# A two-layer hybrid decoder trunk: seven block products instead of eight in the first layer's gate and up projections, with the gated activations kept in DRAM

## The chip, the cores and the metric

The kernel runs on one core of one Trainium2 chip. The core has TensorE (PE, matrix products into PSUM banks), VectorE (DVE), ScalarE (ACT), GpSimd (POOL) and SyncE (SP, which here only issues DMAs). The metric is the device time of one launch in microseconds (us).

## What is computed

The reference is one step of a two-layer decoder for a prompt of 1024 tokens and 8 single-token samples; together they are the 1032 columns (N) that every weight meets. Layer 0 mixes with a short convolution and a gated linear recurrence, layer 1 with latent attention. After each mixer stands a feed-forward stage (the FFN), and the first layer's is what the change is about:

```
def swiglu(h, w_gu, w_down):
    g, u = jnp.split(h @ w_gu, 2, axis=-1)
    return (jax.nn.silu(g) * u) @ w_down
...
hp = modulate(xp, norm_ffn[l], mp[3], mp[4])
...
xp = xp + mp[5] * swiglu(hp, w_gu[l], w_down[l])
```

Here h has 1024 features, w_gu is 1024 x 5632 (gate and up, 2816 columns each), w_down is 2816 x 1024. `modulate` is an RMS norm with a scale and a shift per feature, which come from products of a condition vector with w_ada (the "modulation" below).

## The kernel before

Everything is float32. To get float32 accuracy from TensorE's faster fp32r mode, each operand is split in a high part (a cast) and a low part (the rest), and each product is three matmuls: high by high, high by low, low by high (L2340 to L2342, function `three`). The activations lie transposed: `xT` is 128 partitions x 8 feature tiles (KT) x 1032 columns, `hh` and `hl` are high and low part of the normed input.

**How the first FFN is tiled.** The 1032 columns are three column groups (c = 0, 1, 2) of 344, one PSUM bank each (bank 0, 1, 2). The 5632 gate and up columns are 22 pairs of 128-wide tiles. A *slot* is one weight tile (128 output features) against all columns: 3 groups x 8 feature tiles x 3 matmuls = 72 matmuls of 344 columns. A pair (gate slot, up slot) is 144 matmuls; the text calls it a *tile* of the gate and up product. The stage (`ffn`, called with l = 0) goes through chunks of 6, 6, 5 and 5 tiles (FFN_CHUNKS). After the gate and up slots of a chunk come 8 *down* slots, each with n x 3 x 3 matmuls of 344 columns for the n tiles of the chunk; their result is added to `xT` by DVE (`add_to_x`, L1541 to L1547).

**Who does what in a tile.** SP loads the weights (L515). POOL splits them: cast to `whi` (L746), rest to `wlo` (L748). PE multiplies. ACT takes the gate banks with Silu (L1211), DVE multiplies by the up banks (L1915, `atmp`), ACT casts to `ahi` (L916), POOL makes `alo` (L825). All stay in SBUF. Every engine works through its own list in the order of the program and waits on semaphores; nothing is reordered at run time.

**The modulation of layer 1 rides along.** In the first 12 tiles PE also computes 24 *units* of the second layer's modulation, two in a tile: 16 small matmuls (`ada`, L2459) into bank 4 or 5, ACT copies the result to `adar` (`ada_rows`, L1041), and PE turns it with 2 matmuls each of two passes (`ada_turned`, L2468). In this kernel PE does the `ada` of a slot after column group 0 and the turning after column group 2, so ACT has two column groups of time for the copy.

**The start of the stage.** The output projection of the mixer ends in two slots whose column groups alternate (LAST_PAIR). The squares of `xT` are summed by PE against ones (L2430, L2434), ACT takes the root (L1000), DVE the reciprocal (L1507). Then DVE scales (`htmp`, L1523), ACT adds the shift and casts to `hh` (L1009, L1010), and POOL makes `hl` (L777), feature tile by feature tile; PE starts with the first.

The lines that set the turn-taking on PE are these:

```
def with_ada(i, b, c):
    if c == 0:
        ada(2 * i + 2 * f0 + b, i + f0, b, 1)
    if c == 2:
        ...
        ada_turned(2 * i + 2 * f0 + b, i + f0, b, 1)
```

## Time and profile before

| | us |
|---|---|
| median of three runs | 2955.21 |
| lowest, highest | 2953.56, 2957.14 |
| span of the profiled execution | 2954.8 |

| engine | busy, us | share of the span |
|---|---|---|
| PE, matmuls | 2868.8 | 97% |
| PE, weight loads (PEld) | 2666.3 | 90% |
| DVE | 1087.5 | 37% |
| ACT | 640.8 | 22% |
| POOL | 1037.1 | 35% |

The first FFN begins when the output projection's last product is through (652.47 us from the span's start) and ends at 1459.25 us, where the next stage's first product starts. A matmul's printed duration contains its latency and overlaps the next; how fast matmuls follow each other is read from their starts, or from a stretch's length over their count.

### The profile page before, as it was taken

How to read it: one execution, taken by the hardware profiler on the slowest of the kernel's cores; microseconds unless marked ns; L12 is line 12 of the kernel's file. 1: busy time of each engine (PE TensorE's matmuls, PEld its weight loads, DVE VectorE, ACT ScalarE, POOL GpSimd, SP SyncE). 2: the span in 40 equal slices, each digit the busy share in tenths (PEclk: the TensorE clock that was granted, in tenths of full speed). 3: DMA queues.
4: the chain of work that ended last, by engine and by line, in shares of the span. 5: the costliest groups of instructions: out<-in, count | busy, mean ns of one | idle time of the engine just before them, and what ended most of it. 6: DMA issues, size and time to landing. Idle time of an engine off the chain costs nothing.

```text
span 2954.8 us, 56225 instructions
## 1 busy us (share of the span) xinstructions
PE 2868.8 (97%) x21017; PEld 2666.3 (90%) x21017; DVE 1087.5 (37%) x2298; ACT 640.8 (22%) x1441; POOL 1037.1 (35%) x1060
## 2 busy tenths in 40 slices
PE   6999999999999999999998999999999999999999
PEld 5898998888999999999887787878789999999999
DVE  4767777321020011111436666666650110101103
ACT  5121221223101101001444333332351001000014
POOL 4000000444333334334754333333274334334344
PEclk8999999999999999999999999999999999999999
DMA  7311111453324311111232434343431111111112
GB/s 266 94 44 42 40 45 36 157 165 121 96 75 128 96 47 50 38 54 38 62 105 88 148 97 143 104 136 107 128 113 50 38 49 47 45 50 41 52 42 80
DMA packets 314743, 247.99 MB, mean 84 GB/s; under 512 B 19651, under 2 KB 299062, under 8 KB 313158
## 3 DMA queue, kind: packets, MB, share of 16 engines
q1 hardware_dynamic: 296578, 219.45, 23.9%
q10 hardware_dynamic: 9796, 17.81, 1.7%
q0 software_dynamic: 8192, 8.40, 1.0%
q8 instruction: 107, 1.75, 0.2%
q14 instruction: 70, 0.57, 0.1%
HBM read 222.87 MB, written 22.74 MB: 83 GB/s over the span
## 4 chain that ended last, share of the span: by engine, by line
PE 91%; ACT 2%; DVE 2%; POOL 1%; SPq 1%; issue 1%; DMA 1%; POOLq 0%; DVEq 0%; ACTq 0%
PE bank L2340 24%; PE bank L2342 23%; PE bank L2341 23%; PE bank L2826 2%; PE bank L2945 2%; PE bank L2847 2%; PE bank L2459 1%; POOL hl L777 1%; PE bank L2868 1%; PE bank L2608 1%; PE bank L2580 1%; PE bank L2933 1%; PE bank L2625 1%; SPq L529 1%; PE bank L2815 1%
## 5 line engine op out<-in xcount | busy, mean ns | idle before, releaser
L2340 PE MATMUL bank<-hh,whi 128*128 128x344 f32 (+1 forms) x3468 | 1141.7, 329 | 41.6 <-POOL hl L777 15.0
L2341 PE MATMUL bank<-hl,whi 128*128 128x344 f32 (+1 forms) x3468 | 1115.5, 322 | 0.0
L2342 PE MATMUL bank<-hh,wlo 128*128 128x344 f32 (+1 forms) x3468 | 1115.0, 322 | 0.0
L2340 PEld LDWEIGHTS bank<-hh,whi 128*128 128x128 f32 x3468 | 657.4, 190 | 84.0 <-issue 33.7
L2341 PEld LDWEIGHTS bank<-hl,whi 128*128 128x128 f32 x3468 | 657.3, 190 | 2.5 <-issue 1.1
L2342 PEld LDWEIGHTS bank<-hh,wlo 128*128 128x128 f32 x3468 | 657.2, 190 | 0.6
L746 POOL CAST whi<-wst 128x1024 fp32r<-128x1024 f32 (+4 forms) x222 | 180.6, 813 | 1004.0 <-PE bank L2342 721.8
L1915 DVE TENSOR_TENSOR atmp<-sil,bank 128x344 f32<-128x344 f32 x132 | 67.7, 513 | 938.5 <-PE bank L2342 924.4
L748 POOL TENSOR_TENSOR wlo<-wst,whi 128x1024 fp32r<-128x1024 f32 (+4 forms) x222 | 400.9, 1806 | 17.8
L2340 PE MATMUL bank<-ahi,whi 128*128 128x344 f32 x1056 | 338.7, 321 | 0.0
L2341 PE MATMUL bank<-alo,whi 128*128 128x344 f32 x1056 | 337.4, 319 | 0.0
L2342 PE MATMUL bank<-ahi,wlo 128*128 128x344 f32 x1056 | 337.1, 319 | 0.0
L1211 ACT ACTIVATE sil<-bank 128x344 f32<-128x344 f32 x132 | 60.4, 458 | 963.4 <-PE bank L2342 963.3
L877 POOL DMA_DIRECT2D pr<-in_cache_krope x256 | 139.2, 544 | 219.9 <-issue 215.8
L1543 DVE SCALAR_TENSOR_TENSOR xT<-bank,mod,xT 128x344 f32 (+2 forms) x216 | 123.7, 573 | 220.5 <-PE bank L2342 202.3
L2340 PEld LDWEIGHTS bank<-ahi,whi 128*128 128x128 f32 x1056 | 198.4, 188 | 0.9 <-issue 0.6
L2341 PEld LDWEIGHTS bank<-alo,whi 128*128 128x128 f32 x1056 | 198.4, 188 | 0.1
L2342 PEld LDWEIGHTS bank<-ahi,wlo 128*128 128x128 f32 x1056 | 198.2, 188 | 0.0
L758 POOL TENSOR_TENSOR hl<-xT,hh 128x344 fp32r<-128x344 f32 x24 | 22.3, 963 | 453.7 <-ACT hh L916 453.7
L825 POOL TENSOR_TENSOR alo<-atmp,ahi 128x344 f32 (+1 forms) x132 | 122.5, 929 | 158.3 <-ACT ahi L916 158.3
L916 ACT CAST ahi<-atmp 128x344 f32 (+1 forms) x132 | 63.1, 479 | 299.1 <-DVE atmp L1915 299.1
L1541 DVE TENSOR_TENSOR gtmp<-bank,mod 128x8 f32<-128x8 f32 x72 | 12.0, 167 | 236.2 <-PE bank L2342 236.1
(360 smaller groups left out, 3143.9 us busy)
## 6 DMA issues: line engine op xcount, KB each, us to landing
wst<-in_w_gu SPq DMA_DIRECT2D x88, 512.0 KB
adaw<-in_w_ada SPq DMA_DIRECT2D x40, 1024.0 KB, 5.4
pk<-in_cache_ckv SPq DMA_DIRECT2D x256, 128.0 KB, 2.4
wst<-in_w_in_even SPq DMA_DIRECT2D x28, 512.0 KB
wst<-in_w_down SPq DMA_DIRECT2D x32, 384.0 KB
wst<-in_w_down SPq DMA_DIRECT2D x32, 320.0 KB
adae<-in_w_ada SPq DMA_DIRECT2D x4, 2048.0 KB, 16.2
pr<-in_cache_krope POOLq DMA_DIRECT2D x256, 32.0 KB, 2.3
```

The source lines that it names most:

```text
L746: nc.gpsimd.tensor_copy(whi[b][:, 0:nk, :], wst[b][:, 0:nk, :]).then_inc(w_hi, 1)
L748: nc.gpsimd.tensor_tensor(wlo[b][:, 0:nk, :], wst[b][:, 0:nk, :], whi[b][:, 0:nk, :].bitcast(F), ALU.subtract).then_inc(w_split, 1)
L825: nc.gpsimd.tensor_tensor(d, atmp[c][:], one(ahi[:, bass.ds(i, 1), cols(c)]).bitcast(F), ALU.subtract).then_inc(alo_ready, 1)
L877: pool.dma_start(pr[q][:, j % CG, :], cache_krope[0, bass.ds(page, 1)].rearrange("o p c -> p (o c)")).then_inc(rope_in[q], 16)
L916: nc.scalar.copy(dst, src).then_inc(ready, 1)
L1211: nc.scalar.activation(sil[c][:], bank[c][:, 0:CW], ACT.Silu).then_inc(bank_free[c], 1)
L1543: ins = v.scalar_tensor_tensor(xc, src[:, 0:w], one(gate[:, bass.ds(m, 1), 0:1]), xc, ALU.mult, ALU.add)
L1915: v.tensor_tensor(atmp[c][:], sil[c][:], bank[c][:, 0:CW], ALU.mult).then_inc(act_ready, 1)
L2340: mm(out, wh_, xh_, start=start, stop=False)
L2341: mm(out, wh_, xl_, start=False, stop=False)
L2342: return mm(out, wl_, xh_, start=False, stop=stop)
L2826: ins = nc.tensor.transpose(bank[5][:, (2 * e + ct) * P:(2 * e + ct + 1) * P], page[:, ct * P:(ct + 1) * P], ident[:])
```

## The change

The gate and up product of the first FFN becomes a 2 x 2 x 2 block product by a scheme of Strassen's kind. The blocks of the weights are gate and up (two) by the lower and upper half of the features (two, 4 feature tiles each: KH = 4). The blocks of the activations are the two halves of the features by column *quarters* of 258 (QW = 258): for q = 0 the quarters 0 and 1, for q = 1 the quarters 2 and 3. Seven products P1, P2, P5, P6, P7, P4, P3 (in this order, each for q = 0 and q = 1) take the place of eight; each is 4 feature tiles x 3 matmuls of 258 columns. So a tile is 7 x 2 x 12 = 168 matmuls of 258 columns, where it was 144 of 344.

For that, operands are made that are sums and differences of blocks. On the activations' side this is done once, at the start of the stage, in place in `xT` (`operands` on DVE, `operand_highs` on ACT, `operand_lows` on POOL); the old `xT` is saved to DRAM before and loaded back later. On the weights' side it is done for each tile: DVE makes four sums (`weight_sum`), ACT casts seven 128x512 blocks (`op_high`), POOL makes seven low parts (`op_low`). Behind the products ACT and DVE combine the results (`p1_copy`, `u2_copy`, `u3_copy`, `g1`, `c22`, `g2`), take Silu and multiply, ACT and POOL split the result, and SP stores high and low part to DRAM (`act_high`, `act_low`). All 22 tiles are done before the down product starts; its chunks are now 2, 4, 6, 6 and 4 tiles (DOWN_CHUNKS), loaded back from DRAM (`tile_in`).

Three products share the accumulator `acc_a` (banks 0 and 1), so P7 waits until ACT has copied P6 away, and P4 until ACT has copied P7. The diff, cut to what the following sections speak of:

```
+DOWN_CHUNKS = [(0, 2), (2, 4), (6, 6), (12, 6), (18, 4)]
+QW = N // 4
+KH = KT // 2
+P1, P2, P5, P6, P7, P4, P3 = range(7)
...
+        acc_a, acc_d, acc_b = ([bank[b][:, 0:QW] for b in pair] for pair in ((0, 1), (2, 5), (4, 3)))
+        acc_q = [acc_a, acc_d, acc_b, acc_a, acc_a, acc_a, acc_b]
...
@@ SP @@
+                def cycle(t, ada=False, more=True):
+                    if more:
+                        sp.wait_ge(*op_lo(t.count(7, 7)))
+                        raw_load(l, t.next(2))
+                    for q in range(2):
+                        store(t.next(-1), q)
+                    if ada:
+                        for b in range(2):
+                            load_ada(1, t.at(2, b - 2), b)
...
@@ ACT, in out_proj and behind it @@
+                act.wait_ge(bank_ready[NC - 1], G_OUT + KT + 2)
+                for p in (P7, P4, P3):
+                    op_high(p, first)
...
+            def op_high(p, t):
+
+                if p == P1:
+                    act.wait_ge(*raw_in[t.b](t.loads()))
+                if p in MADE:
+                    act.wait_ge(*s_made(t.count(4, MADE.index(p) + 1)))
+                if not t.first:
+                    act.wait_ge(*block_done[p](t.count(2, 0)))
+                nc.scalar.copy(op_h[p][:], op_source(p, t)).then_inc(op_hi.sem, 1)
...
+                def cycle(t, ada=False, more=True):
+                    gate2(1, t.next(-1))
+                    p1_copy(0, t)
+                    act_high_half(1, 0, t.next(-1))
+                    p1_copy(1, t)
+                    act_high_half(1, 1, t.next(-1))
+                    if more:
+                        op_high(P1, t.next(1))
+                    gate1(0, t)
+                    gate1(1, t)
+                    if more:
+                        op_high(P2, t.next(1))
+                        op_high(P5, t.next(1))
+                    if ada:
+                        ada_rows(t.at(2, ADA_LAYER - 4), 0, 1)
+                    u2_copy(0, t)
+                    u2_copy(1, t)
+                    if more:
+                        op_high(P6, t.next(1))
+                    if ada:
+                        ada_rows(t.at(2, ADA_LAYER - 3), 1, 1)
+                    u3_copy(0, t)
+                    u3_copy(1, t)
+                    if more:
+                        op_high(P7, t.next(1))
+                    act_high_half(0, 0, t)
+                    if more:
+                        op_high(P4, t.next(1))
+                    act_high_half(0, 1, t)
+                    gate2(0, t)
+                    if more:
+                        op_high(P3, t.next(1))
...
+                act.dma_start(xT[:, 5:KT, 0:T], x_rest[:, 5:KT, 0:T]).then_inc(x_in[1].sem, 16)
...
@@ DVE, end of operands (q = 1), and gated @@
+                t1(*quarters[1])
+                t2(*quarters[1])
+                third_out()
+                t3(*quarters[1])
+                t4(*quarters[1])
+                lows(*quarters[1])
...
+                g1(1, t)
+                dve.wait_ge(*t_lo(2 * LOWS))
+                weight_sum(P5, t.next(1))
+                weight_sum(P7, t.next(1))
+                weight_sum(P6, t.next(1))
+                c22(1, t)
...
@@ PE @@
+                else:
+                    pe.wait_ge(*{P6: p1_out, P7: u2_out, P4: u3_out, P3: c22_sum}[p](t.count(2, q + 1)))
+                for j in range(KH):
...
+                    ins = three(acc_q[p][q], op_h[p][:, j, :], op_l[p][:, j, :], t_high[p][:, q, j, :], t_low[p][:, q, j, :],
+                                j == 0 and p in (P1, P2, P5), j == KH - 1, p in (P6, P7, P4, P3))
...
+                def cycle(t, ada_at=None):
+                    for p in range(7):
+                        for q in range(2):
+                            product(p, q, t)
+                        if ada_at is not None:
+                            a, n = t.at(2, -4), t.at(1, -2)
+                            if p == P2:
+                                ada(a, n, 0, 1)
+                            elif p == P5:
...
+                                ada_turned(a, n, 0, 1)
+                                ada(t.at(2, -3), n, 1, 1)
+                            elif p == P6:
+                                ada_turned(t.at(2, -3), n, 1, 1)
```

**How it moves instructions on PE, around a unit of the modulation.** Before, in a tile of the loop, a unit's `ada` is followed by a whole column group of products (24 matmuls) and more before `adar` is turned:

```order
L2342 MATMUL bank<-hh,wlo 128x344
L2456 REGISTER_ALU
L2459 MATMUL bank<-adaw_93,siluc 9x256 x8
L2340 MATMUL bank<-hh,whi 128x344
L2341 MATMUL bank<-hl,whi 128x344
L2342 MATMUL bank<-hh,wlo 128x344
```

Now, in a tile that carries two units (op_h_218 is the high part of P5's weights, op_h_219 of P6's, ada_x the weights of the modulation):

```order
L3038 MATMUL bank<-t_high_203,op_h_218 128x258
L3039 MATMUL bank<-t_low_210,op_h_218 128x258
L3040 MATMUL bank<-t_high_203,op_l_225 128x258
L3162 REGISTER_ALU
L3165 ISA
L3165 MATMUL bank<-sel,adar 128x9
L3165 ISA
L3165 MATMUL bank<-sel,adar 128x9
L3156 MATMUL bank<-ada_x_247,siluc 9x256 x8
L3417 REGISTER_ALU
L3422 REGISTER_ALU
L3038 MATMUL bank<-t_high_204,op_h_219 128x258
```

The first unit's turning now stands directly behind P5's last matmul, and the second unit's `ada` directly behind that.

**And on ACT, in the same place.** Before, in the loop, `adar` is copied right behind the Silu of column group 0:

```order
L1210 ISA
L1211 ACTIVATE sil_79<-bank 128x344
L1039 ISA
L1040 REGISTER_ALU
L1041 COPY adar<-bank 128x256
L1210 REGISTER_ALU
L1211 ACTIVATE sil_80<-bank 128x344
```

Now (L1558 casts the next tile's weights, L1584 copies P6's result, L1357 copies `adar`):

```order
L1558 CAST op_h_217<-raw_230 128x512
L1558 CAST op_h_218<-s_raw 128x512
L1354 ISA
L1355 REGISTER_ALU
L1357 COPY adar<-bank 128x256
L1581 REGISTER_ALU
L1583 REGISTER_ALU
L1584 COPY tq_1_237<-bank 128x258
L1581 REGISTER_ALU
L1583 REGISTER_ALU
L1584 COPY tq_1_239<-bank 128x258
L1558 CAST op_h_219<-raw_230 128x512
```

Each copy of `adar` now stands behind a cast that overwrites the weights of the product that PE has just finished (op_h_218, then op_h_219).

**And on POOL, at the start of the stage.** Before, one weight tile's split stands ahead of the first low part of the input:

```order
L746 CAST whi<-wst 128x1024
L748 TENSOR_TENSOR wlo<-wst,whi 128x1024
L777 TENSOR_TENSOR hl<-htmp_82,hh 128x344
L777 TENSOR_TENSOR hl<-htmp_83,hh 128x344
L777 TENSOR_TENSOR hl<-htmp_84,hh 128x344
```

Now (op_l_227 to op_l_229 are the low weights of P7, P4 and P3, t_low the low parts of the activations' operands):

```order
L1036 TENSOR_TENSOR op_l_227<-raw_first_233,op_h_220 128x512
L1036 TENSOR_TENSOR op_l_228<-raw_first_233,op_h_221 128x512
L1036 TENSOR_TENSOR op_l_229<-raw_first_232,op_h_222 128x512
L1049 TENSOR_TENSOR t_low_208<-xT,t_high_201 128x258 x4
L1053 TENSOR_TENSOR t_low_209<-xT,t_high_202 128x258 x4
L1059 TENSOR_TENSOR t_low_210<-xT,t_high_203 128x1032
L1061 TENSOR_TENSOR t_low_211<-t_raw,t_high_204 128x1032
L1066 TENSOR_TENSOR t_low_214<-xT,t_high_207 128x1032
```

The first low part that PE needs stands behind three low parts of weights, and three of 1032 columns stand behind the eight of 258, once for each q.

## Rows read from the trace of the kernel before

**Rows 1.** The page: the chain that ended last, share of the span by engine.

```profile
PE 91%; ACT 2%; DVE 2%; POOL 1%; SPq 1%; issue 1%; DMA 1%; POOLq 0%; DVEq 0%; ACTq 0%
```

**Rows 2.** Windows (stretch, length, then as headed) of the first FFN's gate and up.

```profile
core 0: us, PE busy (x) PEld busy (x) DVE busy (x) ACT busy (x) POOL busy (x), PEclk, DMA share, GB/s
652.47:821.57 169.10, 161.68 (x1111) 146.96 (x1109) 28.28 (x51) 44.76 (x100) 76.82 (x65) 0.99 0.32 97
889.69:1045.05 155.36, 155.36 (x1106) 145.16 (x1105) 9.72 (x21) 19.60 (x47) 55.64 (x41) 1.00 0.36 109
1113.18:1226.47 113.29, 113.29 (x722) 113.29 (x721) 8.11 (x17) 13.02 (x29) 45.75 (x34) 1.00 0.15 45
```

**Rows 3.** Timeline (start and duration in us) of PE, 256 columns, second layer.

```profile
1737.79 0.28 PE L2340 MATMUL bank<-whi,hh 128*128 128x256 f32 x1
...
1740.29 0.28 PE L2340 MATMUL bank<-whi,hh 128*128 128x256 f32 x1
```

**Rows 4.** Timeline of PE and ACT around a copy of `adar`.

```profile
709.42 0.32 PE L2342 MATMUL bank<-hh,wlo 128*128 128x344 f32 x1
...
709.86 0.46 ACT L1211 ACTIVATE sil<-bank 128x344 f32<-128x344 f32 x1 [8.29 <-PE bank L2342]
710.21 0.37 ACT L1041 COPY adar<-bank 128x256 f32<-128x256 f32 x1
```

**Rows 5.** Timeline of ACT and PE where PE waited for `adar`.

```profile
82.79 0.37 ACT L1041 COPY adar<-bank 128x256 f32<-128x256 f32 x1
...
83.31 0.36 PE L2468 MATMUL bank<-sel,adar 128*128 128x9 f32 x2 [0.86 <-ACT adar L1041]
```

**Rows 6.** Groups by line and shape: count, busy us, mean ns, idle before.

```profile
L916 ACT CAST ahi<-atmp 128x344 f32 x126 | 60.4, 479 | 291.3 <-DVE atmp L1915 291.3
L1102 ACT CAST whi<-wst 128x1024 fp32r<-128x1024 f32 x28 | 29.3, 1046 | 90.2 <-PE bank L2342 90.2
L1258 ACT COPY craw<-bank 128x344 f32<-128x344 f32 x15 | 6.6, 440 | 23.8 <-PE bank L2342 23.8
...
L1686 DVE TENSOR_TENSOR qb<-qb,hq 128x1024 f32<-128x1024 f32 x4 | 4.9, 1226 | 0.1
...
L825 POOL TENSOR_TENSOR alo<-atmp,ahi 128x344 f32 x108 | 100.1, 928 | 123.1 <-ACT ahi L916 123.1
L748 POOL TENSOR_TENSOR wlo<-wst,whi 128x512 fp32r<-128x512 f32 x4 | 5.2, 1288 | 0.3
L748 POOL TENSOR_TENSOR wlo<-wst,whi 128x1024 fp32r<-128x1024 f32 x102 | 244.1, 2393 | 8.2
```

**Rows 7.** Timeline of DVE and PE at the start of the stage.

```profile
652.40 0.42 DVE L1547 TENSOR_TENSOR xT<-xT,gtmp 128x8 f32<-128x8 f32 x1
...
653.25 3.47 DVE L1523 SCALAR_TENSOR_TENSOR htmp<-xT,amp,bank 128x344 f32<-128x344 f32 x7 [0.16 <-DVE mod L1556]
...
657.51 2.30 DVE L1507 RECIPROCAL bank<-rt 128x344 f32<-128x344 f32 x1
...
656.26 0.50 PE L2340 MATMUL bank<-hh,whi 128*128 128x344 f32 x1 [3.50 <-POOL hl L777]
656.55 0.49 PE L2341 MATMUL bank<-hl,whi 128*128 128x344 f32 x1
```

**Rows 8.** Windows, as in rows 2, of the stage's first 19 us.

```profile
656.00:660.00 4.00, 3.74 (x13) 3.22 (x14) 3.66 (x5) 4.00 (x9) 3.94 (x6) 0.57 0.00 0
660.00:675.00 15.00, 11.27 (x60) 6.81 (x59) 10.44 (x18) 11.98 (x26) 9.93 (x11) 1.00 0.37 107
```

**Rows 9.** The page's DMA issues: count, KB each, us to landing.

```profile
x_rest<-xT ACTq DMA_DIRECT2D x15, 516.0 KB, 3.0
xT<-x_rest SPq DMA_DIRECT2D x4, 1548.0 KB, 10.0
xT<-x_rest SPq DMA_DIRECT2D x5, 1032.0 KB, 5.2
```

**Rows 10.** Groups by shape: DVE's add to `xT` behind a down product.

```profile
L1543 DVE SCALAR_TENSOR_TENSOR xT<-bank,mod,xT 128x344 f32 x128 | 73.7, 576 | 175.0 <-PE bank L2342 166.3 <-DVE xT L1547 8.1 <-DVE amp L1559 0.6
```

731 lines of the change are left out of this document (652 added, 79 removed).

## The prediction, made before the changed kernel had run

> **What bounds the kernel now.** The chain that ended last is PE for 91% of the span [rows 1], so PE's time in the changed stretches decides. I read the windows of the first FFN next [rows 2]. Five tiles without modulation units take 113.29 us for 720 matmuls with PE and its weight loads busy throughout: 0.1573 us from matmul to matmul, 22.66 us a tile. Six tiles with units take 155.36 us, or 25.89 a tile, so two units cost 3.23 us of PE. The first six tiles take 169.10 us: the start of the stage costs 13.7 us over that rate. ACT, DVE and POOL are busy for an eighth to two fifths of a steady stretch. The timelines then tell how long a hand from PE to ACT and back takes, which this change puts on the path.
>
> **The products.** The trace has a run of the same fp32r triples at 256 columns: 21 matmuls in 2.50 us, 0.1190 each [rows 3]. From 256 to 344 columns that is 0.00044 us a column, so 258 columns take 0.1199. A tile is 168 x 0.1199 = 20.14 us, 2.52 less than 22.66; over 22 tiles **-55.4 us**. The bounds are close: pure proportion to the columns (0.1180) gives -62, and 0.122 gives -48. The scheme has 168 matmuls where 144 were, so it gains only while a matmul of 258 columns takes under 144/168 of one of 344, or 0.1348 us. At 256 columns the trace is well below that.
> A rule speaks against it: the Trainium skill, page "TensorE: Matmul & The Clock Gate", section "Back-to-back issue gap", gives a sustained stream of weight load and matmul as about 81 ns at 128 columns and 131 ns at 512. As an estimate from that page, 344 columns would take 109 ns and 258 columns 98 ns, a tile would go from 15.7 to 16.5 us, and the products would cost 16 us more in all. This trace disagrees at both widths (157 and 119 ns), so I go by the trace.
>
> **The steady tile, other engines.** A product of one q is 12 x 0.12 = 1.44 us. P7 of a q waits for ACT's copy of P6 of that q, and one product of the other q lies between. The hand over is: ACT starts 0.44 us after the start of PE's last matmul, 0.28 after PE would go on [rows 4]; the copy of 258 columns takes 0.37 (440 ns at 344 [rows 6], 0.37 at 256 [rows 4]); PE starts 0.15 after ACT's end [rows 5]. That is 0.80 of the 1.44 there are, so it is hidden if ACT's list is not late. Seven casts of 512 (0.62, between 479 ns at 344 and 1046 at 1024), and fourteen operations of 258 at some 0.4, are 10 us of 20; POOL's seven low parts at 1.29 and four at 0.75 are 12 us; DVE's are 7. I walked the three lists once round the tile and found no PE wait. The four DVE sums and the low parts have most of a tile of time. Cost **0**, and 0.5 to 1 us a tile if the cover of 0.64 us is gone (below). The stores and reloads of the activations (1 MB a tile each way) use a DMA that is busy for 0.36 of the time with units running [rows 2]: 0.
>
> **The units of the modulation.** This is what eats the gain. PE turns the first unit directly behind P5, and the copy that it waits for stands in ACT's list behind the cast of the next tile's P5 weights, which itself may not start before P5 of this tile is done. So PE waits: 0.28 to ACT, 0.51 from the start of the cast to that of the copy (0.62 less the 0.11 by which operations overlap: 0.46 long, 0.35 apart [rows 4]), 0.37 the copy, 0.15 back: 1.31 us. The second unit's copy stands behind the copy of P6 for q = 1 (0.26) and the cast of P6: 1.57 us. Before, a column group of 3.8 us covered this copy. In the 12 tiles with units that is 12 x 2.88 = **+34.6 us**. Bounds: 12 x 2.4 if the turning's own start is absorbed in the wait, 12 x 3.4 if ACT's register instructions add to each step: +29 to +41. A tile with units then takes 20.14 + 3.23 + 2.88 = 26.2 us, no better than the 25.9 before.
>
> **The start of the stage.** Now P1 needs only one quarter, but everything behind it is a chain over three engines. On ACT, casts for P7, P4 and P3 stand behind the last square; on POOL their low parts (3 x 1.29) push the first low part of the input to 659.1, against 656.26 [rows 7]. Then POOL sets the pace: 8 x 0.75 until P2 ends at 664.8. For P5, ACT has to finish 16 casts and shifts (0.40 each), 4 shifts and a copy before the 1032-column cast (1.05), POOL takes 2.41 for its low part: 668.9. P6 needs another 2.41. Then P7 and P4 each wait 0.8 for a copy; q = 0 ends at about 678.6. For q = 1 DVE has a reciprocal (2.30 [rows 7]) and eight scalings (0.49 apart) left, ACT follows at 0.80 a feature tile until 685.5, P2 ends at 686.7. Then POOL has two low parts of the next tile's weights ahead of the 1032-column one: P5 starts at 693.2, P6 ends at 697.0. The copy that P7 waits for stands behind ACT's cast of the next P5 weights, this behind DVE's `weight_sum`, this behind `dve.wait_ge(*t_lo(2 * LOWS))`, that is behind POOL's last 1032 columns at 697.9: P7 starts at 700.2. The tile ends at 705.4, and I add 0.6 for matmuls at half the clock behind the idle gaps: after the 3.5 us gap the clock stood at 0.57 [rows 8] and matmuls came 0.29 apart [rows 7]. Cost over a plain tile: 706.0 - 652.47 - 20.14 = 33.4, against 13.7 before: **+19.7 us**. Bounds: +8 (each link 15% shorter, the last one hidden) to +32.
>
> **The down product.** The same matmuls, so 0 in itself. With chunks of 2 a slot is 18 x 0.157 = 2.83 us, and DVE needs three adds of 0.58 [rows 10] and some 0.5 for the samples: hidden. At its start DVE is late by the last sums, the modulation's 1.2 us and so on, about 3.2 us: PE waits some 1.1 us at the second slot. Rows 5 to 7 of `xT` come back only after the last store has landed (about 3 us [rows 9]); they are 1.5 MB, and such loads took 5.2 to 10.0 us [rows 9], so they land 13 to 18 us into the down product, and slot 4 needs them at 13.4, slot 5's banks at 15.3. Together **+2 us** (1 to 5).
>
> **The sum.** -55.4 + 34.6 + 19.7 + 2 = +0.9 us on the profiled span of 2954.8, which is 0.4 below the median of the runs. So 2955.7 + 0.4 = **2956 us**. The seven-product scheme saves 55 us of matmuls and gives them back at the start of the stage and in the waits for `adar`.
>
> **Rivals.**
> 1. *The start is cheap.* If the engines' lists overlap better than in my walk, because q = 0's products already run while operands are made, the start costs +8 and the units +30: -55.4 + 30 + 8 + 2 = -15, **2940 us**. For it: ACT, DVE and POOL were busy 60 to 80% of the first 15 us [rows 8], not all of it. Against: each link that I counted is an instruction with a row. Chance 0.28.
> 2. *ACT's list is late in the steady tile* (the slower side). ACT takes casts, Silus and copies in a fixed order, and a copy of P6 or P7 that ends over 1.44 us after its product stops PE. It decides as soon as something ahead of `u2_copy` or `u3_copy` holds ACT for over 0.64 us, one cast's length. At 1 us a tile for 22 tiles this is +22: **2978 us**. For it: six hands from PE to ACT and back in 20 us where there were three in 26. Against: by my walk ACT is free before each of them. Chance 0.30, with a start of the stage at its upper bound counted here.
> 3. *The clock falls in the stage again and again.* The matmuls after the 3.5 us gap ran at 1.2 instead of 2.4 GHz; but with PE waiting half a microsecond at each feature tile afterwards the clock stood at 1.00 [rows 8]. Waits of 1.3 and 1.6 us are between. If they halve the clock for some 3 us each, it is 24 x 1.5 = +36: **2992 us**, chance 0.05.
> 4. *Matmuls of 258 columns are not cheaper* than 0.1348, from a fixed cost that 256 columns don't show: products +0, total +56: **3011 us**, chance 0.02. By the Trainium skill's figures above, the same sum would end at some 3027.
>
> **How the numbers follow.** The forecast, the parts cancelling, has 0.35. About 0.2% (5.9 us) is what a measurement of this kernel can tell from no change. Of the forecast's chance some falls on each side of that bound; with the rivals I get faster 0.31, same 0.33, slower 0.36. For the range, the bounds of the four terms (-62 to -48, 29 to 41, 8 to 32, 1 to 5) taken together give 2934 to 2983; with rival 2 inside it and rivals 3 and 4 outside, about 0.2 is left out.
>
> **What would show it.** In the profile after: (1) matmuls of 258 columns 0.119 to 0.121 us apart, and tiles without units 20.1 us each; (2) in each tile with units two PE waits for ACT `adar`, 1.3 and 1.6 us, before L3165; (3) the first tile ends about 53 us after the output projection, with PE waits of 4 us before P5 of q = 0 and 6.5 us before P5 of q = 1; (4) PE waits of 1 to 4 us in the first down chunk. A steady tile clearly over 20.2 us, waits for `tq` or `u3` in the loop, or no wait before L3165 would make it wrong.

## The result, and the profile after

| | runs | median us | range | profiled execution | its span | granted clock |
|---|---|---|---|---|---|---|
| before | 4 | 2956.18 | 2953.56 to 2957.77 | 2955.2 | 2954.8 | 0.988 |
| changed | 4 | 2998.28 | 2993.12 to 3006.16 | 3006.16 | 3004.1 | 0.975 |

The changed kernel is slower: its time is 1.0148 of before, 95% interval 1.013 to 1.0165, some 42 us where 0 were forecast, and outside the range of 2934 to 2983. The two profiled spans lie 49.3 us apart, since the profiled execution of the changed kernel is its slowest. This is how the difference spreads over the stretches of the two traces (after minus before, in us):

| stretch | forecast | traces | |
|---|---|---|---|
| output projection, before the stage | 0 | +4.8 | ends at 657.3, was 652.5 |
| products of 22 tiles | -55.4 | -53.9 | 20.21 us a plain tile, was 22.66 |
| units of the modulation, 12 tiles | +34.6 | +46.2 | 85.0 us over plain tiles, were 38.8 |
| start of the stage | +19.7 | +33.4 | 67.35 us to tile 1, less a plain tile 47.1, were 13.7 |
| down product | +2 | +16.3 | 271.98 us, was 255.72 |
| behind it | 0 | +2.4 | |
| sum | +0.9 | +49.2 | |

PE still holds most of the chain that ended last, but DVE and "issue" have doubled against [rows 1], and ACT went from 2% to 3%:

```profile
PE 87%; DVE 4%; ACT 3%; issue 2%; SPq 1%; DMA 1%; POOL 1%; DVEq 0%; ACTq 0%; POOLq 0%
```

The windows of the changed kernel, in the order first tile, twelve tiles with units, eight plain tiles, down product (compare [rows 2]):

```profile
core 0: us, PE busy (x) PEld busy (x) DVE busy (x) ACT busy (x) POOL busy (x), PEclk, DMA share, GB/s
657.30:724.65 67.35, 37.54 (x174) 34.13 (x173) 56.43 (x77) 37.03 (x74) 39.72 (x33) 0.67 0.11 36
744.96:1072.46 327.50, 293.87 (x2499) 271.77 (x2497) 97.35 (x168) 116.91 (x276) 147.89 (x132) 0.97 0.49 156
1072.46:1234.16 161.70, 161.70 (x1346) 161.70 (x1345) 61.79 (x108) 70.15 (x162) 93.02 (x86) 1.00 0.40 130
1234.16:1506.14 271.98, 258.51 (x1598) 252.79 (x1597) 104.10 (x215) 17.43 (x36) 104.86 (x103) 0.99 0.37 126
```

The third row is the part that came as forecast: PE busy throughout at clock 1.00, 161.70 us for 8 x 168 matmuls, 0.1203 each. In the first row DVE is busy for 56 of 67 us and PE for little over half, at a granted clock of 0.67: a mix of its two levels, 2.4 and 1.2 GHz. A matmul of 258 columns comes 0.12 us after the one before at the higher level and 0.215 at the lower.

Next comes the timeline of ACT and PE in a tile with units, around the second unit. ACT goes from the cast of the next tile's weights straight to the copy of `adar`, and PE, which waits for that copy, stands idle for 1.42 us. That figure starts at the printed end of PE's last matmul. The next one could have started 0.16 us earlier, so the wait costs 1.58 us; the waits of the units are counted this way below. All twelve tiles have two such waits, 37.5 us in all:

```profile
760.77 0.38 ACT L1584 COPY tq<-bank 128x258 f32<-128x258 f32 x1 [1.06 <-PE bank L3040]
761.04 0.62 ACT L1558 CAST op_h<-raw 128x512 fp32r<-128x512 f32 x1
761.56 0.38 ACT L1357 COPY adar<-bank 128x256 f32<-128x256 f32 x1
762.08 0.58 PE L3165 MATMUL bank<-sel,adar 128*128 128x9 f32 x4 [1.42 <-ACT adar L1357]
```

Now the timeline of DVE and POOL in the first tile. DVE's `t3` (L2453, four operations of 258 columns with two inputs in SBUF) takes 7.51 us beside three subtractions of POOL. By the single operations: 2.24, 2.60 and 2.42 us while POOL works, and 0.47 for the last, with POOL idle.

```profile
672.39 7.51 DVE L2453 SCALAR_TENSOR_TENSOR xT<-xT,mod 128x258 f32<-128x258 f32 x4
672.16 2.19 POOL L1059 TENSOR_TENSOR t_low<-xT,t_high 128x1032 fp32r<-128x1032 f32 x1 [3.62 <-ACT t_high L1622]
674.40 2.46 POOL L1061 TENSOR_TENSOR t_low<-t_raw,t_high 128x1032 fp32r<-128x1032 f32 x1
676.83 2.38 POOL L1066 TENSOR_TENSOR t_low<-xT,t_high 128x1032 fp32r<-128x1032 f32 x1
```

The same happens in the down product and at its end. The add of the samples' 8 columns (L2041, also two inputs in SBUF) starts after POOL's subtraction has started and ends 0.02 to 0.03 us after it, and PE waits for the add, directly or through ACT's `atmp`. With no POOL operation beside it the add takes 0.16.

```profile
1265.40 1.26 POOL L960 TENSOR_TENSOR wlo<-wst,whi 128x512 fp32r<-128x512 f32 x1
1265.48 1.20 DVE L2041 TENSOR_TENSOR xT<-xT,gtmp 128x8 f32 x1
1266.73 0.42 PE L3038 MATMUL bank<-down_high,whi 128*128 128x344 f32 x1 [1.25 <-DVE xT L2041]
...
1500.88 2.34 POOL L960 TENSOR_TENSOR wlo<-wst,whi 128x1024 fp32r<-128x1024 f32 x1
1501.28 1.97 DVE L2041 TENSOR_TENSOR xT<-xT,gtmp 128x8 f32<-128x8 f32 x1
...
1503.83 0.84 PE L3130 MATMUL bank<-atmp,ones 128*128 128x344 f32 x2 [2.49 <-ACT atmp L1245]
```

Last, the output projection, which the forecast had not looked at. SyncE's queue issues the loads of `raw_first` ahead of a load of output weights. POOL waits 12.17 us for these weights, ACT's square waits for POOL, and PE waits for the copy behind the square.

```profile
602.66 1.93 SPq L681 DMA_DIRECT2D raw_first<-in_w_gu  x2
604.71 2.71 SPq L620 DMA_DIRECT2D wst<-in_w_out_even  x1
612.91 1.04 POOL L958 CAST whi<-wst 128x1024 fp32r<-128x1024 f32 x1 [12.17 <-DMA wst<-in_w_out_even]
617.35 0.49 ACT L1245 ACTIVATE sq<-xT 128x344 f32<-128x344 f32 x1 [14.28 <-POOL acce L981]
618.46 0.61 PE L3165 MATMUL bank<-sel,adar 128*128 128x9 f32 x4 [3.52 <-ACT adar L1357]
```

### The profile page after: what moved, and what is told of

Its sections match the earlier page's. It is cut to its first block, busy times and chain, and to the rows that moved or that the text cites. A ratio compares the mean times of both kernels' runs of the same rounds, so it can differ in the third digit from the quotient of the medians.

```text
span 3004.1 us, 58789 instructions
## 1 busy us (share of the span) xinstructions
PE 2847.3 (95%) x21545; PEld 2640.4 (88%) x21545; DVE 1293.6 (43%) x2615; ACT 785.1 (26%) x1772; POOL 1105.8 (37%) x1162
## 4 chain that ended last, share of the span: by engine, by line
PE 87%; DVE 4%; ACT 3%; issue 2%; SPq 1%; DMA 1%; POOL 1%; DVEq 0%; ACTq 0%; POOLq 0%
PE bank L3038 23%; PE bank L3039 22%; PE bank L3040 22%; PE bank L3594 2%; PE bank L3713 2%; PE bank L3615 2%; PE bank L3156 1%; PE bank L3636 1%; PE bank L3305 1%; PE bank L3277 1%; PE bank L3701 1%; PE bank L3322 1%; PE bank L3165 1%; SPq L634 1%; POOL hl L989 1%
## 5 line engine op out<-in xcount | busy, mean ns | idle before, releaser
L3038 PE MATMUL bank<-hh,whi 128*128 128x344 f32 (+2 forms) x2412 | 799.7, 332 | 33.9 <-POOL wlo L960 7.7
L3039 PE MATMUL bank<-hl,whi 128*128 128x344 f32 (+2 forms) x2412 | 780.1, 323 | 0.0
L3040 PE MATMUL bank<-hh,wlo 128*128 128x344 f32 (+2 forms) x2412 | 779.9, 323 | 0.0
L3038 PEld LDWEIGHTS bank<-hh,whi 128*128 128x128 f32 (+1 forms) x2412 | 459.9, 191 | 61.3 <-issue 23.8
L3039 PEld LDWEIGHTS bank<-hl,whi 128*128 128x128 f32 (+1 forms) x2412 | 460.2, 191 | 2.4 <-issue 1.0
L3040 PEld LDWEIGHTS bank<-hh,wlo 128*128 128x128 f32 (+1 forms) x2412 | 460.4, 191 | 0.6
L3038 PE MATMUL bank<-t_high,op_h 128*128 128x258 f32 x1232 | 363.8, 295 | 29.8 <-POOL t_low L1059 11.0
L3039 PE MATMUL bank<-t_low,op_h 128*128 128x258 f32 x1232 | 357.8, 290 | 0.0
L3040 PE MATMUL bank<-t_high,op_l 128*128 128x258 f32 x1232 | 356.5, 289 | 0.0
L960 POOL TENSOR_TENSOR wlo<-wst,whi 128x1024 fp32r<-128x1024 f32 (+5 forms) x186 | 297.5, 1599 | 14.9
```

What stands on the lines that cost most here:

```text
L960: nc.gpsimd.tensor_tensor(wlo[b][:, 0:nk, :], wst[b][:, 0:nk, :], whi[b][:, 0:nk, :].bitcast(F), ALU.subtract).then_inc(w_split, 1)
L3038: mm(out, wh_, xh_, start=start, stop=False, skip_group_check=more)
L3039: mm(out, wh_, xl_, start=False, stop=False, skip_group_check=more)
L3040: return mm(out, wl_, xh_, start=False, stop=stop, skip_group_check=more)
```

## The experiments

First, the changed kernel was measured again, with no edit.

> The changed kernel once more, with no edit, so that the experiments of this call have it beside them on the same chip: 2993 to 3003, about 1.4 to 1.6% over before. If it stands at 2994 to 2996, the small gains of the other edits (DVE's low parts, chunks of 4) were nothing; if it stands at 3000 or over, they were some 4 us.

Measured: 3001.72 us (2998.20 to 3003.49), 1.0156 of before. Up to the end of the first layer its stretches are those of the first trace within 0.4 us; behind it this trace is 2.8 us shorter (1495.14, was 1497.92). The two medians of this one kernel differ by 3.4 us, so gains of 1 to 5 us are read from the traces below. By their ratios to before, the runs of DVE's low parts (1.0147) and of the chunks of 4 (1.0152) can't be told from the changed kernel (1.0148 and 1.0156).

One more reading guards against small differences. The part of the program behind the first layer is the same in all these kernels, and took 1489.73 us in one profiled run and 1497.49 in another (of two experiments further down); PE's busy time differs as much, 1449 and 1457, and the granted clock over the whole run was 0.984 in the first and 0.980 in the second:

```profile
1431.07:2920.80 1489.73, 1449.20 (x11136) 1335.65 (x11136) 567.95 (x1307) 382.51 (x914) 614.19 (x704) 0.99 0.27 83
```

```profile
1425.71:2923.20 1497.49, 1457.01 (x11136) 1343.48 (x11136) 568.05 (x1307) 382.24 (x914) 614.07 (x704) 0.99 0.27 83
```

### The copies for the units

In ACT's `cycle`:

```
                         op_high(P2, t.next(1))
+                    if ada:
+                        ada_rows(t.at(2, ADA_LAYER - 4), 0, 1)
+                    if more:
                         op_high(P5, t.next(1))
                     if ada:
-                        ada_rows(t.at(2, ADA_LAYER - 4), 0, 1)
+                        ada_rows(t.at(2, ADA_LAYER - 3), 1, 1)
                     u2_copy(0, t)
...
                         op_high(P6, t.next(1))
-                    if ada:
-                        ada_rows(t.at(2, ADA_LAYER - 3), 1, 1)
```

> Edit: on ACT, the copies of the modulation's rows (`ada_rows`) go ahead of the casts of the next tile's P5 and P6 weights; nothing else. Theory (the copies stand in ACT's list behind casts that wait for the very product behind which PE turns the rows): all 24 PE waits before L3165 (37.5 us in all, 1.2 to 1.7 us each in the changed kernel) go, and with them the five stretches at half the clock behind them (3.4 us), so the twelve tiles with units fall from 26.3 to 28.3 us to about 23.4 each, and the kernel from 2998 to about 2955 (2952 to 2960). Rival A (the waits only move, to PE's waits for the copies of P6 and P7, because ACT's list is full there): gain under 15 us, new waits at L3038 to L3040. Rival B (the clock is what costs, whatever the waits): tiles of 28.2 us stay beside shorter ones.

Measured: 2952.43 us, 0.9998 of before (0.9988 to 1.0007), 46 us under the changed kernel. The twelve tiles take 279.21 us, 23.27 each, at clock 1.00; there is no wait before the turning, and no tile of 28 us:

```profile
740.29:1019.50 279.21, 279.21 (x2499) 261.87 (x2498) 97.36 (x168) 118.16 (x276) 148.60 (x132) 1.00 0.58 183
```

```profile
747.63 0.36 ACT L1357 COPY adar<-bank 128x256 f32<-128x256 f32 x1
750.37 0.62 ACT L1558 CAST op_h<-s_raw 128x512 fp32r<-128x512 f32 x1 [2.37 <-PE bank L3041]
```

The copy now stands 2.7 us ahead of the cast that held it, and no wait came in its place: rival A is out. The order of two entries in ACT's list was worth 48.3 us of this stretch, as much as the whole loss. Of it 37.5 are the waits, and some 7.5 are stretches at half clock: five tiles (28.2 and 27.9 us where the others have 26.7 and 26.3) are 1.5 us longer each. The remaining 3.3, or 0.3 a tile, are slower starts of the matmuls right behind a wait. In the changed kernel's trace each of the five stretches stands behind the second wait of its tile (1.58 to 1.76 us), and none behind a first wait (1.24 to 1.47); this is so in all ten traces that have the waits. (The 3.4 in the expectation is about the length of one such stretch, 3.2 to 3.5, not the sum of what they cost, so the theory was right and its price for the clock too small.)

### The port that DVE and POOL share

> Edit: the three low parts of 1032 columns that POOL makes for each quarter pair at the start of the stage (L1059, L1061, L1066: subtractions of two SBUF operands) are replaced by memsets of the same tiles to zero, so this part of the result is left out (the low parts of the inputs of P5, P6 and P3). POOL writes as much, and reads nothing. Theory (DVE's operations with two SBUF inputs and POOL's operations with SBUF inputs take turns at a common port, each for its whole length): DVE's four L2453 operations take 0.47 each, 1.9 for the four, instead of 7.5 and 7.1, and P7 of q = 0 starts about 5.5 us earlier. Rival A (any POOL work slows DVE, by its writes too): they still take about as long as the POOL operation beside them. Rival B (DVE is slow there for a reason of its own, the operand's place or a wait that the trace counts as busy): L2453 stays at 7 us for four.

Measured: 2984.39 us (one run). DVE and POOL at the place shown above:

```profile
672.53 1.67 DVE L2455 SCALAR_TENSOR_TENSOR xT<-xT,mod 128x258 f32<-128x258 f32 x4
672.28 0.96 POOL L1048 MEMSET t_low<- 128x1032 f32 x1 [3.61 <-ACT t_high L1624]
```

`t3` takes 1.67 instead of 7.51, and its first two operations take 0.48 each, though they run while POOL is writing the same bytes as before. So POOL's reading of SBUF is what DVE waited for; rivals A and B are out. In q = 1, `t3` took 3.04: its first operation fell beside POOL's low part of a weight, a subtraction. P7 of q = 0 starts 21.0 us after DVE's first scaling of the stage, 26.8 in the changed kernel. (The first tile is 14 to 17 us shorter in all, but a memset is also less than half as long as the subtraction, so that is no price for the port alone.)

The Trainium skill, page "SBUF — State Buffer", section "SBUF: two separate sides", has this as a rule: a port pair of DVE and GpSimd is an exclusive lock for the whole instruction, and a DVE operation with two SBUF inputs contends for it, though only against a GpSimd operation that reads SBUF. The traces agree: 0.47 us alone, 2.24 to 2.60 beside a subtraction and 0.48 beside a memset. The rule also covers casts on POOL, and the trace of before shows this: the add that took 0.42 us in [rows 7] ends 0.02 us after a cast of POOL, and all 21 adds of that kernel that took over 0.2 us end so.

```profile
651.76 1.04 POOL L746 CAST whi<-wst 128x1024 fp32r<-128x1024 f32 x1 [6.29 <-issue]
```

It was a rule that spoke against this change, and the prediction had not weighed it.

Then the same low parts by DVE itself, which leaves POOL idle there:

```
# POOL, operand_lows: the subtractions for t_low[P5], t_low[P6], t_low[P3] are gone
# DVE, between t2 and t3:
+  dve.wait_ge(*t_hi(HIGHS * q + HIGH_T1))
+  v.tensor_tensor(t_low[P5][:, q], xT[:, 0:KH, here], t_high[P5][:, q].bitcast(F), ALU.subtract)
+  dve.wait_ge(*t_hi(HIGHS * q + HIGH_T2))
+  v.tensor_tensor(t_low[P6][:, q], t2_raw[:], t_high[P6][:, q].bitcast(F), ALU.subtract)
# and behind P4's low part the same for P3; ACT casts t_high[P3] last
```

> Edit: at the start of the stage those three low parts are made by DVE (P5's and P6's ahead of its `t3`, P3's last) instead of POOL, and ACT casts P3's operand last; the result is whole. Theory (port taken in turns, and the chain DVE, ACT, POOL is what PE waits for): a low part takes 1.23 on DVE against 2.2 to 3.1 on POOL, the four L2453 take 1.9 instead of 7.5, P7 of q = 0 starts some 5 us earlier, the first tile (67.4 us from the end of the output projection to tile 1) shortens by 12 to 16 us, the kernel from 2998 to 2982 to 2987. Rival A (the half clock sets the tile's time): under 4 us. Rival B (DVE becomes the queue that all wait for, since it gains 6 x 1.23 us of work): P5 of both quarters starts later than now, and the gain is under 6 us.

Measured: 2996.95 us, 1.0147 of before (1.0127 to 1.0167). `t3` takes 1.67 us as forecast, but it starts 2.3 us later, since DVE's two new low parts stand ahead of it. P7 of q = 0 starts only 2.6 us earlier, and tile 1 starts 61.8 us after DVE's first scaling instead of 67.2 (64.9 to 67.2 over seven runs, below): 3 to 5 us, not 12 to 16. The gain is as small as rival B had it, but not for its reason: P5 of both quarter pairs starts earlier, not later (16.2 us after the first scaling instead of 17.0, and 42.7 instead of 47.9). The lock was priced right and the chain wrong: the last long wait of the tile, 5.4 us before P7 of q = 1, is still there, and the experiment on ACT's list in the first tile finds its cause.

### The clock in the first tile

```
+    def again(n, dst):        # spare products, operands ready since long
+        pe.wait_ge(*op_lo(7))
+        for _ in range(n):
+            for j in range(KH):
+                three(dst, op_h[P3][:, j, :], op_l[P3][:, j, :], t_high[P1][:, 0, j, :], t_low[P1][:, 0, j, :], j == 0, j == KH - 1)
     product(P2, q, t, low(P2, KH))
+    again((2, 4)[q], acc_b[q])
...
     product(P6, q, t)
+    pe.wait_ge(*g1_sum(1))
+    again((3, 3)[q], acc_d[0])
```

> Edit: in the first tile PE runs spare products (of operands that stand ready, into a bank that the next product clears) before P5 (2 and 4 times a product's 12 matmuls) and before P7 (3 each), where it waits for operands now. Nothing is left out; 144 matmuls are added. Theory A (the chain over DVE, ACT and POOL sets the first tile, the half clock adds some): the products behind the spare ones take 1.4 instead of 2.4 to 2.5 us; six or seven of them stand one behind another on the path, so the first tile is 4 to 8 us shorter. Theory B (the clock is off the path): within 1 us of the changed kernel. Rival C (spare products run over the end of the wait, themselves at half clock at 2.5 us each): longer by up to 4 us.

Measured: 2998.55 us, 3.2 under the changed kernel beside it, with ranges that overlap. Windows of the first tile, first with spare products, then without:

```profile
656.10:722.38 66.28, 49.30 (x319) 44.94 (x318) 57.45 (x77) 37.10 (x74) 38.82 (x32) 0.87 0.11 36
```

```profile
657.40:724.99 67.59, 38.54 (x176) 34.92 (x175) 56.72 (x77) 37.05 (x74) 39.66 (x33) 0.67 0.11 34
```

The clock rises from 0.67 to 0.87 and the tile gets 1.3 us shorter. That lies between theories A and B, nearer to B: most products at half clock (2.6 us instead of 1.4) end in a wait for DVE or ACT anyway. But this run does not price the clock at the tile's end. There PE still waited 2.05 us before P7 of q = 1, and 27 of the last 36 matmuls ran at 1.2 GHz. What that is worth is seen in seven profiled runs of kernels whose first tile has no edit. Tile 1 starts 64.9 to 65.0 us after DVE's first scaling in the four whose last two products ran at full clock, 66.6 in one whose last product did in part, and 67.2 in the two where neither did. So the clock at the end alone makes 2.3 us, and it falls differently from run to run though the first tile's code is the same.

### ACT's list in the first tile

ACT's list behind the operands of q = 1, in `gated` (the Silu of `gate1` also goes behind the first copy):

```
                 gate2(0, t)
-                op_high(P5, t.next(1))
-                gate1(1, t)
                 u2_copy(1, t)
-                op_high(P6, t.next(1))
+                gate1(1, t)
                 u3_copy(1, t)
+                op_high(P5, t.next(1))
+                op_high(P6, t.next(1))
                 op_high(P7, t.next(1))
```

> Edit: on the changed kernel, in the first tile, ACT's copies of P6 and P7 of q = 1 go ahead of its casts of the next tile's P5 and P6 weights; nothing else. Theory (the step of the prediction): ACT is free for the copy at 710.6 instead of 715.4, P7 of q = 1 starts near 711.1 instead of 715.9, 58.4 to 58.7 us behind DVE's first scaling of the stage becomes 53.5 to 54.5, and the first tile shortens by 4 to 5 us. Rival (DVE's low part of P7, 3.2 us late beside POOL, or tile 1's own P5 then waits for the late casts): under 2 us.

Measured: 2993.53 us (one run). ACT takes the copy right behind its casts, and PE's P7 starts at 710.76, within 0.4 us of the forecast:

```profile
708.99 1.06 ACT L1632 CAST t_high<-xT 128x1032 fp32r<-128x1032 f32 x1
709.95 0.41 ACT L1596 ACTIVATE tq<-tq 128x258 f32<-128x258 f32 x1
710.27 0.35 ACT L1584 COPY tq<-bank 128x258 f32<-128x258 f32 x1
```

P7 starts 53.6 us after the first scaling, 58.5 without the edit. Tile 1 starts 61.9 us after it, 3.0 to 5.3 less than in those seven runs. Not all of the 4.9 need arrive, because P4 then waits for the copy of P7, which stands behind a Silu, and that behind DVE's 3.24 us low part beside POOL. So this step of the prediction was right as a mechanism.

### The samples' add

```
-    order(v.tensor_tensor(gtmp[:], src[:, w:CW], one(gate[:, bass.ds(m, 1), 1:1 + NS]), ALU.mult))
+    order(v.tensor_tensor(src[:, w:CW], src[:, w:CW], one(gate[:, bass.ds(m, 1), 1:1 + NS]), ALU.mult))
...
-    ins = v.tensor_tensor(xs, xs, gtmp[:], ALU.add)
+    ins = v.tensor_tensor(xs, xs, src[:, w:CW], ALU.add)
```

> Edit: in `add_to_x`, the product of the samples' columns with their gate stays in the bank (PSUM) instead of `gtmp` (SBUF), so that the 8-column add has one SBUF input instead of two; the result is whole. It stands in every down product and in the output projection. Theory (that add, 0.16 us alone, lasts 0.46 to 1.97 us beside a subtraction on POOL, and PE waits for it): the add takes under 0.25 everywhere; the 0.65 us pauses at the turns of the loops over 4 tiles (7 of them) go; in the chunk of 2 the slots come down from 3.1 to 3.2 us towards 2.83; and the 2 us at the end of the stage go: 6 to 12 us in all. Rival A (the add is not what PE waits for, the turn of a loop costs 0.65 us by itself): the pauses stay, under 2 us gained. Rival B (a write to a bank costs DVE more than one to SBUF): the product takes over 0.3 us, and nothing is gained.

Measured: 2990.27 us, 1.0122 of before (1.0106 to 1.0137), 11.5 under the changed kernel beside it. The two blocks show the add in the changed kernel, and then with the edit (groups by line: count, busy us, mean ns of one):

```profile
L2041 DVE TENSOR_TENSOR xT<-xT,gtmp 128x8 f32 (+1 forms) x80 | 33.7, 421 | 0.0
```

```profile
L2041 DVE TENSOR_TENSOR xT<-xT,bank 128x8 f32 (+1 forms) x80 | 12.2, 152 | 0.0
L2035 DVE TENSOR_TENSOR bank<-bank,mod 128x8 f32<-128x8 f32 x80 | 14.0, 175 | 241.0 <-PE bank L3040 240.7
```

The pauses at the turns of the loops over 4 tiles are gone. There were six, each with 0.65 us between two matmuls where 0.16 is usual, so they had cost 0.5 each. The down product takes 264.24 us instead of 271.97: 3 us are the pauses, 2.5 come from the chunk of 2, some 2 from the end of the stage. So the edit itself is worth 7.7 us by the traces. The rest of the 11.5 is not its doing, as far as the traces tell: the end of the first tile ran at full clock here (2.3 us), and the stretches before and behind differ as they do between runs. In the chunk of 2, PE lost 11.0 us in the changed kernel and still 8.5 with this edit, so the add is the smaller part of that loss.

> Edit: the kernel before the change (eight products), with the samples' product kept in the bank in `add_to_x`, so that the add there has one SBUF input. In this kernel the add took 201 ns in the mean (421 in the changed kernel, 152 with the edit), so it has met a subtraction on POOL seldom. Theory: within 0.15% of before (under 4 us), so the 11 us that the edit gave the changed kernel were a cost of its chunks of 2 and 4 tiles. Rival: before loses as much to these meetings, unseen, and gains 8 us or more.

Measured: 2954.80 us, 1.0001 of before (0.9991 to 1.0011). Its add takes 152 ns in the mean, 201 before the edit, where the changed kernel has 421. So the cost belongs to the changed kernel's chunks of 2 and 4. In its own chunks of 6 the add met no operation of POOL (0.16 us each), and no turn paused.

### The chunks of the down product

```
-DOWN_CHUNKS = [(0, 2), (2, 4), (6, 6), (12, 6), (18, 4)]
+DOWN_CHUNKS = [(0, 4), (4, 4), (8, 4), (12, 6), (18, 4)]
```

with the reloads of the activations moved to match.

> Edit: the down product's chunks hold 4, 4, 4, 6 and 4 tiles instead of 2, 4, 6, 6 and 4. The products are the same; a slot of the first chunk has twice the matmuls. Theory (in the chunk of 2, DVE's 3.1 to 3.2 us a slot is longer than PE's 2.83, and it starts late): with 5.7 us a slot DVE is hidden, the down product shortens by 8 to 11 us from 272.0, PE waits once for the late start (2 to 3 us), the kernel from 2998 to 2987 to 2990. Rival (the loss is in data that comes late: the rows of `xT`, or the tiles that the first chunk now also needs): a wait of the same size stands at the first slots of the longer chunk, and nothing is gained or up to 5 us is lost.

Measured: 2996.98 us, 1.0152 of before (1.0132 to 1.0172). A miss: the down product takes 269.85 us, 2.1 less. The first chunk's loss is down to two long waits. One for DVE costs 0.9 us, and one costs 2.5 and is for POOL's split of a down weight whose load came late, so the rival had a part of it. But 13 turns of a loop over 4 tiles now have the pause where 6 had it, which the timeline of PE, DVE and POOL explains:

```profile
1266.58 1.29 POOL L962 TENSOR_TENSOR wlo<-wst,whi 128x512 fp32r<-128x512 f32 x1
1266.66 1.23 DVE L2043 TENSOR_TENSOR xT<-xT,gtmp 128x8 f32 x1
1267.95 0.43 PE L3040 MATMUL bank<-down_high,whi 128*128 128x344 f32 x1 [0.34 <-DVE xT L2043]
```

This row led to the edit of the samples' add above; the two are put together below.

### The order of two loads in the output projection

```
     for b in range(2):
         load(2 * i + G_OUT + b, b, wst[b][:], ...)
+        if b == 0 and i is KT // 2 - 1:      # stood ahead of this pair's first load
+            for z in range(2):
+                sp.dma_start(raw_first[z][:], gate_up(0)[:, :, z, 0, :]).then_inc(raw_in[0].sem, 16)
```

> Edit: of the changed kernel, SyncE issues the two loads of the first tile's gate and up columns (`raw_first`, 1 MB) behind the next load of output projection weights instead of ahead of it. Theory (the output projection ends 4.8 us later than before, since that load of weights comes in behind 1 MB, and POOL's split, ACT's square and PE's turning wait for it): the PE wait of 3.8 us near 614.6 falls under 1.5, and the output projection ends at 652.5 to 654.5 instead of 657.3. Rival (those waits come from the loads of the modulation's weights, which took 6 to 10 us each there): the wait moves by one slot and the end stays at 656 or later.

Measured: 2992.66 us (one run). DVE's first scaling of the stage starts at 652.42 us (657.42 in the changed kernel), the first product at 658.62.

> The same edit as in the look before (the two loads of `raw_first` behind the next load of weights), alone on the changed kernel, timed. Theory (the order of the loads costs the output projection 5 us): 2993 to 2997, 1.3 to 1.4% over before, first product of the stage near 658.6 where the changed kernel has 663.6 to 664.0. Rival (the look caught a lucky landing, loads vary from run to run): 3000 to 3002, the output projection's end as in the changed kernel.

Measured: 2993.85 us, 1.0125 of before (1.0108 to 1.0142); first product at 659.04. POOL has the weights 3.5 us earlier, and the wait of PE before L3165 there (3.52 us in the changed kernel) is gone:

```profile
609.39 1.04 POOL L959 CAST whi<-wst 128x1024 fp32r<-128x1024 f32 x1 [8.64 <-DMA wst<-in_w_out_even]
```

DVE's first scaling starts at 652.83 instead of 657.42. It starts at 655.2 to 659.1 us in the twelve traces with the old order and at 652.1 to 654.4 in the five with the new one, 4.5 us apart in the mean. The order of the two loads is therefore the +4.8, with a spread of some 2 us from run to run.

### Together

Three edits at once (units, low parts on DVE, samples' product in PSUM):

> The three edits together: the copies of the modulation's rows ahead of the casts, the low parts at the start of the stage on DVE, and the samples' product in PSUM. If their gains add up (46 us by the run of the first against the changed kernel, some 5 by the trace of the second, 6 to 12 for the third): 2935 to 2942, 0.4 to 0.6% faster than before. If the changed scheme's start is bound otherwise and the pauses stay: 2949 to 2953, the same as before.

Measured: 2939.95 us, 0.9947 of before (0.9933 to 0.9961). The gains add up.

Then less work for DVE in the first tile:

```
# POOL, q == 0, behind P2's low parts: low parts of P4 and P3 (DVE keeps P5, P6, P7)
# DVE:
+                rs2 = column_roots(inst, 2)
                 second_out()
-                rs2 = column_roots(inst, 2)
```

> Edit: on top of the three edits, the low parts of P4 and P3 of the first quarter pair go back to POOL, which makes them while DVE scales with one input in PSUM, and DVE's last reciprocal goes ahead of its sum for P3. Theory (DVE, busy 51 of 62 us there, bounds the first tile, and it takes no turns with POOL while an input of its is in PSUM): DVE's scaling at L2434 keeps its 0.49 us beside POOL's subtractions of 2.3 us, the products of q = 1 start 3 to 4 us earlier, 2936 to 2938. Rival (the turns come back, or P4 and P3 wait for POOL, PE works in order and q = 1 starts no earlier): 2939 to 2943.

Measured: 2935.19 us, 0.9934 of before (0.9917 to 0.9951). Eight scalings with an input in PSUM take 2.52 us beside POOL's subtraction as without it:

```profile
680.28 2.52 DVE L2432 SCALAR_TENSOR_TENSOR xT<-xT,amp,bank 128x172 f32<-128x172 f32 x8
...
680.32 2.19 POOL L1061 TENSOR_TENSOR t_low<-xT,t_high 128x1032 fp32r<-128x1032 f32 x1 [10.13 <-ACT t_high L1627]
```

P1 of q = 1 starts 30.6 us after the first scaling, 32.9 in the run before, which is 2.3 earlier where 3 to 4 were forecast. The tile is 2.7 us shorter.

Then the casts and low parts of the first weights of P7, P4 and P3 behind the operands of q = 0:

> Edit: on top of that, the casts and low parts of the first tile's weights of P7, P4 and P3 go behind the operands of the first quarter pair (ACT had 1.6 us of them and POOL 3.75 ahead of the first operand). Theory (three engines stand in one chain from the last square on): P1 and P2 of q = 0 end 2 to 3 us earlier, P5 of q = 0 starts 1 to 2 us earlier, 1 to 2 us less in all than the run before. Rival (DVE's scaling and reciprocal set P5's start, whatever stands ahead on ACT and POOL): only P1 and P2 move, the time stays within 1 us of the run before.

Measured: 2935.93 us, 0.9938 of before (0.9923 to 0.9952). P5 of q = 0 starts 15.6 us after the first scaling, 16.2 without the edit, and tile 1 0.6 us earlier: near the rival, DVE's own operations set this start.

All edits so far, with the later loads and the chunks of 4:

> All edits together: the five of the start and the units that gave 2935 to 2936, the later loads of `raw_first`, and the chunks of 4, 4, 4, 6, 4 in the down product, now with the samples' product in PSUM. Theory (chunks of 4 gained nothing because each turn of a loop over 4 tiles paused 0.65 us behind the samples' add, and that is gone): the down product falls from 257.3 (end of the products to the end of the last column group but one) to 252 to 254, with no pause at the turns; with 5 us from the loads: 2924 to 2928, 0.9 to 1.0% faster than before. Rival (the first slots wait for the tiles that the longer chunk needs, or the loads' gain does not add): 2930 to 2936.

Measured: 2925.05 us, 0.9898 of before (0.9881 to 0.9914). First tile, tiles with units, plain tiles, down product:

```profile
652.80:710.86 58.06, 35.45 (x173) 32.61 (x174) 48.55 (x79) 37.16 (x74) 30.77 (x29) 0.71 0.13 40
731.40:1010.60 279.20, 279.20 (x2498) 261.86 (x2497) 97.54 (x168) 118.56 (x276) 146.07 (x132) 1.00 0.58 183
1010.60:1172.30 161.70, 161.70 (x1346) 161.70 (x1345) 61.84 (x108) 70.33 (x162) 93.32 (x87) 1.00 0.40 129
1172.30:1431.41 259.11, 254.10 (x1599) 251.68 (x1597) 86.69 (x215) 17.46 (x36) 104.30 (x103) 1.00 0.39 130
```

No pause at a turn is left. The chunks of 4 now take 4.9 us off the down product, which was 264.0 in the three runs before; with the pauses it was 2.1. The down product is 3.4 us over that of the kernel before. The wait for POOL's split of a weight in the third slot, 2.5 us in the run of the chunks alone, is still in it, and no run isolates its cause.

> On top of all edits: ACT's casts of the next tile's P1 and P2 weights (1.14 us), and so POOL's two low parts of them, go behind the operands of the second quarter pair. Theory (ACT's P5 operand and DVE's low part of P6, 2.3 instead of 1.23 us beside POOL, are on the path of the first tile): P7 of q = 1 starts about 2 us earlier and the time falls by 1.5 to 2.5 us against the run before. Rival (the next tile's P1 then waits for POOL): tile 1 starts no earlier, same time or up to 1 us more.

Measured: 2923.21 us, 0.9897 of before (0.9880 to 0.9913). The low part of P6 takes 1.23 us as meant, yet P7 of q = 1 starts 49.6 us after the first scaling, 49.5 without the edit. Tile 1 does start 2.1 us earlier, but only because the last two products ran at full clock in this trace. So the theory missed, though the time fell about as forecast. ACT's list shows why: the cast waits for `weight_sum` and the copy stands behind it:

```profile
702.67 0.62 ACT L1558 CAST op_h<-s_raw 128x512 fp32r<-128x512 f32 x1 [1.81 <-DVE s_raw L2387]
703.20 0.41 ACT L1577 ACTIVATE tq<-tq 128x258 f32<-128x258 f32 x1
703.52 0.36 ACT L1584 COPY tq<-bank 128x258 f32<-128x258 f32 x1
```

> The same order of ACT's list on top of the run before last (all edits, and the casts of P1 and P2 behind the operands): ACT comes to the copy at 700.8 instead of 703.5 there, so P7 of q = 1 and tile 1 start 2.5 to 3 us earlier: 2920 to 2921, 1.1% faster than before. Rival (tile 1 then waits for its P5 or P6 weights): 2923 to 2925.

Measured: 2922.69 us, 0.9891 of before (0.9875 to 0.9908). Tile 1 starts 53.3 us after the first scaling instead of 56.1, 2.8 us earlier as forecast; the median moved by 0.5. These are the two runs whose unchanged later part differed by 7.8 us (the windows at the head of this section), so the time can't show it; the trace does.

## Why the prediction was wrong

By stretches the forecast missed +49.2 by 48.3 us: 14.3 in the down product, 13.7 at the start of the stage, 11.6 in the units, 4.8 in the output projection, 2.4 behind the first layer (which is within the spread between runs) and 1.5 in the products. The first three terms all lie past their bounds.

**The products** were right: 0.1203 us a matmul against 0.1199 from [rows 3], -53.9 against -55.4. The Trainium skill's figures for such a stream (page "TensorE: Matmul & The Clock Gate", section "Back-to-back issue gap") had given an estimate of 98 ns at 258 columns. These operands don't bear it out at this width either: 120 ns.

**The units** were right in mechanism and too small. The waits were 1.24 and 1.58 us in the first of the twelve tiles against 1.31 and 1.57 forecast, but 1.44 and 1.73 inside the hardware loops. That is 3.17 a tile, inside the bounds of 2.4 and 3.4. What the term put at nothing are the stretches at half clock: rival 3 had them behind every wait or none, and they came behind 5 of 24, 7.5 us in all. The experiment took 48.3 us out of this stretch by the order of a list.

**The start of the stage** measured +33.4 against +19.7, past its bound of 32. Shifted by the 4.8 us of the output projection, the walk gave the end of P2 within 0.4 us (669.6, was 669.2) and P5 of q = 0 within 0.7 (673.7, was 674.4). The step that failed is the next, "Then P7 and P4 each wait 0.8 for a copy". P7 waited from 679.6 to 684.3: `t3` ended at 679.9, the cast and the low part of P7 behind it at 682.2, and the copy that P7 also needs at 684.1. On ACT that copy stands behind P4's cast, a table load of 1.28 us that the walk did not have, and a Silu:

```profile
681.07 1.05 ACT L1632 CAST t_high<-xT 128x1032 fp32r<-128x1032 f32 x1
682.14 1.28 ACT L1577 ACT_TABLE_LOAD   x1
...
683.76 0.36 ACT L1584 COPY tq<-bank 128x258 f32<-128x258 f32 x1
684.26 0.55 PE L3038 MATMUL bank<-t_high,op_h 128*128 128x258 f32 x1 [4.33 <-ACT tq L1584]
```

DVE's sums were taken as hidden at the length that they have alone, and took 5.8 and 5.4 us more in the two quarter pairs (7.51 and 7.11 against 1.67). Of the 13.7 us, 7.3 are lost by the end of q = 0's products (690.7, where the shifted walk has 683.4). By the start of P7 of q = 1 it is 10.9 (715.9, walk 705.0): `t3` was held again, and POOL's last subtraction, which starts behind DVE's sums, took 3.1 us beside DVE where the walk had 2.4. The last 3 us are the clock: the last three products ran at 1.2 GHz, 2.6 us each instead of 1.4, where the prediction had added 0.6 in all. The trace of before did hold a hint of the lock, the 0.42 us of the samples' add in [rows 7], where the same operation took 0.16 at other times. The last long wait, before P7 of q = 1, was named rightly and is shown by its own run.

**The down product**: "DVE needs three adds of 0.58 [rows 10] and some 0.5 for the samples: hidden" is the step that failed, together with the single wait of 1.1 us at the second slot. The eight slots of the chunk of 2 took PE 33.6 us where its matmuls need 22.6: 11.0 lost, 4.6 of it in the first two slots. A slot took DVE 3.0 to 3.3 us with the waits between its operations and the samples' add at 0.46, against PE's 2.83. With the add at 0.15 DVE needs 2.7 a slot, and still 8.5 us were lost there; only the longer chunk took them away, so the short slot itself was the larger cause, and which hand-over between PE and DVE makes it no run isolates. To this came 3 us in six pauses at turns of the loops over 4 tiles, and 2 us at the end of the stage. With the add in PSUM and chunks of 4 the term is +3.4, inside the bounds of 1 to 5.

**The output projection** was left out: the loads of `raw_first` were counted at nothing, and no queue that they pass was named. They stand ahead of a load that PE's chain waits for, and that made 4.8 us.

**The rivals.** None of them gave this result. Rival 1 (a cheap start) and rival 4 (no cheaper matmuls) are refuted by the start's +33.4 and by 0.1203 us a matmul. Rival 2 (ACT late in the steady tile, 0.30) did not happen as told, since plain tiles are at PE's bound; the start past its upper bound, which was counted with it, did. Rival 3 came true in a fifth of its places. ACT's list was late at the units and in the first tile, where its entries wait for the very product behind which PE needs a copy.

So the scheme's saving of 54 us is real and was lost around it. With the lists in another order, longer first chunks and fewer meetings of DVE and POOL, the kernel with seven products runs 1.1% under the kernel before. Of these edits only the samples' add was also tried on the kernel before, where it gave nothing.

## What to carry to other kernels

Before a step of an in-order engine's list is placed, ask what the entry ahead of it waits for: a copy that another engine needs must not stand behind a cast that waits for the very same product. Count DVE operations with two inputs in SBUF at the length of the POOL subtraction or cast beside them, however small they are, and give them an input in PSUM or another time. A saving in the steady state is spent first at the seams, so price the first tile, the last one and the stage before as carefully as the loop.

## What the runs showed of the hardware

- A DVE operation with two SBUF inputs that meets a POOL subtraction is held until this ends: 8 columns took 1.97 us instead of 0.16, 258 columns 2.60 instead of 0.47. Beside a POOL cast it is the same: in the kernel before, 8 columns took 0.21 to 0.50 us and ended 0.02 to 0.03 after the cast. Beside a POOL memset of 1032 columns they were not held (0.48 each). A scaling with one input in PSUM was not held beside a subtraction either (2.52 us for eight).
- In the tiles with units, stretches at 1.2 GHz came behind 5 of the 12 second waits of a tile (1.58 to 1.76 us) and behind none of the 12 first waits (1.24 to 1.47); a tile lost 1.5 us by one. With no such wait in the stretch the clock stood at 1.00.
- In the first tile 128 of 168 matmuls ran at 1.2 GHz, and 92 to 141 in the seven traces without an edit there. Spare products raised the clock from 0.67 to 0.87 and won 1.3 us, but left the last three products mostly at 1.2 GHz; the last two at full clock are worth 2.3 us.
